# A hybrid decoder layer on one core: the last quarter of attention's loads at unit 28, first cached values behind blocks, a third block result buffer

## The reference, cut to what matters

```
PATTERNS = ((128, 1), (512, 4), (2048, 16))          # window, dilation
s = einsum(q, k) * scale + bias[t5_bucket(rel * dil)]  # masked: 0 <= rel <= span
m = max(s); pr = exp(s - m); den = sum(pr)
o = pr @ v / den;  lse = m + log(den)
out = sum(softmax(stack(lse)) * stack(o))              # over the three patterns
# sample: keys and values = cache (2048 rows) followed by the 8 new rows
```

## Time and profile before

| | us |
|---|---|
| median of three runs (lowest, highest) | 2499.04 (2494.27, 2503.16) |
| span of the profiled execution | 2491.6 |
| PE busy (share of the span) | 2197.5 (88%) |
| DVE, ACT, POOL busy | 851.4, 564.0, 288.6 |
| mean of the 16 DMA engines | 176 GB/s |

### The profile page before, as it was taken

How to read it: one execution, slowest core, us unless ns; L and a number is a source line. 1 busy time by engine, 2 the same in 40 slices (tenths; PEclk the granted TensorE clock), 3 DMA queues, 4 the chain that set the end, 5 groups by cost and what they waited for, 6 DMA issues and landing times. The chain is left out here.

```text
span 2491.6 us, 27646 instructions
## 1 busy us (share of the span) xinstructions
PE 2197.5 (88%) x7615; PEld 1096.3 (44%) x7616; DVE 851.4 (34%) x1969; ACT 564.0 (23%) x1111; POOL 288.6 (12%) x463
## 2 busy tenths in 40 slices
PE   4996999998896577899999749999999999999995
PEld 1343555444453244455544324444444444444442
DVE  4566643036542223454566531111111111111111
ACT  3410101235532122333432201111111111111111
POOL 0001020001001010000021121111111111111111
PEclk8998999999997677899999969999999999999998
DMA  9152141433448543222244344676659788687873
GB/s 378 74 216 49 54 91 40 149 101 98 139 156 213 165 152 155 67 85 83 79 160 178 103 166 155 226 254 193 197 174 344 259 322 320 220 327 274 292 266 69
DMA packets 122756, 438.91 MB, mean 176 GB/s; under 512 B 31955, under 2 KB 70579, under 8 KB 102115
## 3 DMA queue, kind: packets, MB, share of 16 engines
q1 hardware_dynamic: 92520, 309.99, 34.0%
q0 software_dynamic: 26032, 112.64, 16.7%
q10 hardware_dynamic: 4112, 15.14, 1.5%
HBM read 356.39 MB, written 83.10 MB: 176 GB/s over the span
## 5 line engine op out<-in xcount | busy, mean ns | idle before, releaser
L2528 PE MATMUL bank<-arena 128*128 128x512 f32 x1120 | 492.1, 596 | 14.4 <-issue 14.4
L2179 PE MATMUL bank<-arena 128*128 128x512 f32 (+1 forms) x960 | 359.7, 534 | 9.6 <-ACTq L1050 9.6
L2528 PEld LDWEIGHTS bank<-arena 128*128 128x128 f32 x1120 | 212.4, 190 | 290.2 <-issue 290.2
L2556 PE MATMUL bank<-arena 128*128 128x512 f32 x560 | 250.4, 600 | 9.4 <-issue 9.4
L2179 PEld LDWEIGHTS bank<-arena 128*128 128x128 f32 x960 | 168.7, 192 | 194.4 <-issue 193.5
L2433 PE MATMUL bank<-arena 128*128 128x512 f32 x512 | 248.5, 615 | 2.2 <-DMA arena<-mix_d 2.2
L2071 DVE COPY arena<-bank 128x512 f32<-128x512 f32 x50 | 34.6, 693 | 548.7 <-PE bank L2543 548.7
L2556 PEld LDWEIGHTS bank<-arena 128*128 128x128 f32 x560 | 103.6, 190 | 133.3 <-issue 130.3
L2338 PE MATMUL bank<-arena 128*128 128x64 f32 x568 | 95.5, 301 | 41.1 <-DVEq L1810 27.9
L2433 PEld LDWEIGHTS bank<-arena 128*128 128x128 f32 x512 | 90.2, 193 | 76.5 <-issue 74.0
L2081 DVE TENSOR_TENSOR arena<-bank,arena 128x512 f32<-128x512 f32 (+1 forms) x50 | 34.5, 690 | 256.4 <-PE bank L2556 208.6
(11 more groups left out here) (476 smaller groups left out, 2548.7 us busy)
## 6 DMA issues: line engine op xcount, KB each, us to landing
arena<-wg SPq DMA_DIRECT2D x32, 2048.0 KB
arena<-wu SPq DMA_DIRECT2D x32, 2048.0 KB, 15.2
arena<-wd SPq DMA_DIRECT2D x32, 2048.0 KB, 8.6
arena<-mod_w SPq DMA_DIRECT2D x12, 2048.0 KB, 18.3
z_d<-arena ACTq DMA_DIRECT2D x12, 1056.0 KB, 6.5
arena<-z_d POOLq DMA_DIRECT2D x10, 1056.0 KB, 7.6
arena<-kc POOLq DMA_DIRECT2D x8, 1280.0 KB, 8.4
arena<-vc POOLq DMA_DIRECT2D x8, 1280.0 KB, 8.0
```

Of the source, the lines that this page charges most:

```text
L2179: ins = mm(bank[n % 2][:, 0:w], wz[:, i % 3, k, :], hT[:, k, t0:t0 + w], start=(k == 0), stop=(k == KT - 1))
L2528: ins = mm(bank[bk][:, :], xgT[:, s, k, :], m[w][:, k, :], start=(k == 0), stop=(k == KT - 1))
L2556: ins = mm(bank[4 + h][:, :], hhT[:, k, :], wd[w][:, k, 512 * h:512 * h + 512], start=(k == 0), stop=(k == 3))
```

## The change

- `ldq 3`, the last quarter of queries, keys and values, moves from behind the barrier into the slot of unit 28. It waits in addition for `t1_ready`, since part of `v1` first holds a bias table.
- `ost` gets a third tile, in the place of a weight that is no longer needed (`gatew`). `att_max` of block b now waits for the store of block b-3, and there is a third semaphore, `st_att2`; the reader of `att_d` waits for all three.
- POOL's loads stand in another order: keys 2 and 3 come ahead of values 0 and 1, and these two wait until one and two blocks more are done (`att_o` of 2 and 3).

```diff
--- before.py
+++ after.py
@@ -136,6 +136,7 @@
             a, w = VCOLS[name]
             return vec[:, a:a + w] if i is None else vec[:, a + i:a + i + 1]
 
+        gatew_at = top[0]
         gatew = take(4 * P).rearrange("p (n m) -> p n m", n=4)
         lg = take(NT * 36).rearrange("p (i n) -> p i n", i=NT)
         zero = lg.rearrange("p i n -> p (i n)")[:, 0:512]
@@ -191,7 +192,8 @@
         top[0] = h_at
         ssb = take(2048).rearrange("p (n k) -> p n k", n=4)
         pt = take(2048).rearrange("p (n k) -> p n k", n=4)
-        ost = take(2 * 264).rearrange("p (n h c) -> p n h c", n=2, h=4)
+        ost = [take(264), take(264), take(264, gatew_at)]
+        ost = [o.rearrange("p (h c) -> p h c", h=4) for o in ost]
         kc_at = top[0]
         wo = take(8192).rearrange("p (k n) -> p k n", k=KT)
         kc = take(2 * 2560, kc_at).rearrange("p (n h k) -> p n h k", n=2, h=2)
@@ -328,7 +330,7 @@
                     *tile(3), ("tabs", 0), ("Ap", 0), ("As", 0), *tile(4), *tile(5), ("A", 1), ("Aw", 1), *tile(6), ("tabs", 1), ("Ap", 1), ("As", 1), *tile(7),
                     ("sqA",), ("B", 0), *tile(8), ("outA",), ("outAn",), *tile(9), ("tabs", 2), ("B", 1), *tile(10), ("sqB",), *tile(11), ("outB",),
                     ("outBn",), *tile(12), *tile(13), ("ldq", 0), *tile(14), ("ldq", 1), ("t1p",), *tile(15), ("ldq", 2), *tile(16), *tile(17), *tile(18),
-                    ("bar", 1), ("ldq", 4), ("ldq", 3), ("smp",)]
+                    ("bar", 1), ("ldq", 4), ("smp",)]
 
         BLOCKS = []
         for c in range(4):
@@ -346,7 +348,7 @@
         VPART = ((0, 4), (4, 8), (8, 11))
 
         def sample(u):
-            out = [("qb",)] if u == 4 else []
+            out = [("qb",)] if u == 4 else [("ldq", 3)] if u == 28 else []
             if u in (28, 56):
                 out.append(("so", u // 28 - 1))
             hf, n = divmod(u, 28)
@@ -624,6 +626,8 @@
 
             def ldq(step, c):
                 t0, w = CHUNKS[c]
+                if c == 3:
+                    sp.wait_ge(S("t1_ready"), 1)
                 if c == 0:
                     sp.wait_ge(S("st_mixd"), 16 * 6)
                     for h in range(4):
@@ -646,7 +650,7 @@
                 if u % 4 == 3:
                     bk = u // 4
                     sp.wait_ge(S("att_o"), bk + 1)
-                    sp.dma_start(att_rows(bk), ost[:, bk % 2].rearrange("p h c -> p (h c)")).then_inc(S(f"st_att{bk % 2}"), 16)
+                    sp.dma_start(att_rows(bk), ost[bk % 3].rearrange("p h c -> p (h c)")).then_inc(S(f"st_att{bk % 3}"), 16)
 
             def smp_out(step, hf):
                 sp.wait_ge(S("smp_o"), hf + 1)
@@ -657,8 +661,8 @@
                 if i >= 2:
                     sp.wait_ge(S("mrg_o"), i - 1)
                 if i < NT - 1:
-                    for q in range(2):
-                        sp.wait_ge(S(f"st_att{q}"), 64 * (i // 4 + 1))
+                    for q in range(3):
+                        sp.wait_ge(S(f"st_att{q}"), 16 * len(range(q, 8 * (i // 4 + 1), 3)))
                     sp.dma_start(ma[:, i % 2].rearrange("p q h c -> p q (h c)"),
                                  att_d[:, t0:t0 + P].rearrange("q t c -> t q c")).then_inc(S(f"ld_ma{i % 2}"), 16)
                 else:
@@ -871,6 +875,8 @@
                 def values(b):
                     if b >= 2:
                         pool.wait_ge(S("smp_pv"), b - 1)
+                    else:
+                        pool.wait_ge(S("att_o"), 2 + b)
                     pool.dma_start(vc[:, b % 2], A["vc"][b]).then_inc(S(f"ld_vc{b % 2}"), 16)
                     pool.dma_start(vn[0:8, b % 2], O["v"][TP + 8 * b:TP + 8 * b + 8]).then_inc(S(f"ld_vc{b % 2}"), 16)
                 def tables():
@@ -883,7 +889,7 @@
                 keys(0)
                 keys(1)
                 tables()
-                for f, b in ((values, 0), (values, 1), (keys, 2), (keys, 3), (keys, 4), (keys, 5), (values, 2), (values, 3),
+                for f, b in ((keys, 2), (keys, 3), (values, 0), (values, 1), (keys, 4), (keys, 5), (values, 2), (values, 3),
                              (values, 4), (values, 5), (keys, 6), (keys, 7)):
                     f(b)
                 pool.dma_start(rw, A["rw"]).then_inc(S("ld_wo"), 16)
@@ -1214,8 +1220,8 @@
             def att_exp(step, u):
                 w = 128 * len(BLOCKS[u // 4][4])
                 act.wait_ge(S("att_max"), u + 1)
-                link(act.activation(ssb[:, u % 4, 0:w], ssb[:, u % 4, 0:w], ACT.Exp, bias=ost[:, (u // 4) % 2, u % 4, 64:65], scale=-1.0,
-                                    accum_out=ost[:, (u // 4) % 2, u % 4, 65:66]))
+                link(act.activation(ssb[:, u % 4, 0:w], ssb[:, u % 4, 0:w], ACT.Exp, bias=ost[(u // 4) % 3][:, u % 4, 64:65], scale=-1.0,
+                                    accum_out=ost[(u // 4) % 3][:, u % 4, 65:66]))
                 act.sem_inc(S("att_exp"), 1)
 
             def att_turned(step, u):
@@ -1783,12 +1789,12 @@
                 if u == 0:
                     dve.wait_ge(S("ld_t1"), 16 * 8)
                     dve.wait_ge(S("t1_ready"), 1)
-                if u % 4 == 0 and u >= 8:
-                    dve.wait_ge(S(f"st_att{(u // 4) % 2}"), 16 * (u // 8))
+                if u % 4 == 0 and u >= 12:
+                    dve.wait_ge(S(f"st_att{(u // 4) % 3}"), 16 * (u // 12))
                 if u >= 4:
                     dve.wait_ge(S("att_pT"), u - 3)
                 dve.wait_ge(S("att_s"), u + 1)
-                m = ost[:, (u // 4) % 2, u % 4, 64:65]
+                m = ost[(u // 4) % 3][:, u % 4, 64:65]
                 link(dve.tensor_tensor_reduce(out=ssb[:, u % 4, 0:w], in0=bank[u % 2][:, 0:w], in1=tab[:, tab.shape[1] - w:],
                                               scale=-1.0, scalar=3e38, op0=ALU.add, op1=ALU.min, accum_out=m))
                 dve.sem_inc(S("att_max"), 1)
@@ -1806,7 +1812,7 @@
                 if u % 4 == 3:
                     bk = u // 4
                     dve.wait_ge(S("att_pv"), u + 1)
-                    link(dve.tensor_copy(ost[:, bk % 2, :, 0:64], bank[4][:, 0:256].rearrange("p (h c) -> p h c", h=4)))
+                    link(dve.tensor_copy(ost[bk % 3][:, :, 0:64], bank[4][:, 0:256].rearrange("p (h c) -> p h c", h=4)))
                     dve.sem_inc(S("att_o"), 1)
 
             def sample_queries(step):
```

## The result

The changed kernel took 2477.16 us, the median of four runs (2469.26 to 2479.55), beside 2501.1 us of the kernel before on the same chip: ratio 0.9903, 95% interval 0.9884 to 0.9922, some 24 us less. A second set of runs on another occasion gave 2469.09 beside 2499.8 us, 0.9871 (0.985 to 0.9892). The profiled span went from 2491.6 to 2473.0 us, and in the second pair of profiles from 2487.7 to 2470.5 us: 18.6 and 17.2 us, less than the medians say. The kernel before was profiled at the quick end of its runs both times: its second profiled run took 2489.42 us, while none of the seven runs beside it was under 2495.54.

What follows compares the result with a forecast made beforehand. It took PE's 21.89 us stand before unit 8, for block 0's store behind the seven loads, as the one large gap. 20.9 + 2.0 + 3.1 = 26.0 us off 2499.0 gave 2473 us, range 2462 to 2488.

Steps and rivals of the forecast that it cites:

- The gap before unit 8: Before unit 8's transposes, PE idle 21.89 us for block 0's late store; moved loads and third tile save 20.9 us.
- the twin: Units 36 to 41, same work as units 8 to 13: 19.00 us against 39.90, so the store cost 20.9 us.
- Keys 0 and 1: PE's 2.04 us wait for cached keys at 808.30 us goes once the seven loads are away: 2.0 us saved.
- Keys 2 and 3 ahead of the values: Next in line at unit 11; landing as keys 6 and 7 do, 8.9 us, already in the 19.00 us: nothing added.
- The waits of values 0 and 1: Value 1, issued after block 2, lands by 871.5 us, wanted at 873.56: costs nothing, 2 us or more to spare.
- The seven loads at unit 28: Done near 913 us, block 6's store near 915, wanted at unit 36 by 921.2: 6 us slack, no cost.
- rival A: Stall moves to unit 36, block 6's store behind the seven loads: up to 18 us, likely 2482 us; chance 0.10.
- Later blocks: Third tile removes the 1.55 and 1.57 us waits before the transposes of units 32 and 56: 3.1 us saved.
- Rival C: With fewer idle stretches, two of four windows reach full clock: 8.6 us more saved, 2464 us; chance 0.07.
- B: Gap shrinks but keys 2 and 3 or value 1 land late: 5 to 10 us come back, 2481; chance 0.08.
- D: Slower than before: loads at unit 28 starve stores, units 36 and 40 both wait, up to 2509 us; chance 0.03.
- The signs: Right if no att_d wait over 2 us before unit 56, store 0 landing under 8 us, units 8 to 13 18–21 us.

Runs made afterwards that it cites:

- e1: Kernel before with only the seven loads moved to unit 28, two tiles, POOL's old order: units 0 to 56 177.9 us, ratio 0.9952.
- e3: Kernel before with only POOL's new order and its waits, loads at the barrier, two tiles: units 0 to 56 184.9 us, ratio 0.9976.
- e7: Changed kernel with the seven loads at unit 6, right behind the store of block 0: units 0 to 56 173.1 us, ratio 0.9924.
- e5: Changed kernel without the third tile: units 0 to 56 170.4 us, ratio to the kernel before 0.9949.
- e6: Changed kernel with POOL's old order, without the waits on blocks: units 0 to 56 169.8 us, ratio to the kernel before 0.9927.
- e8: Changed kernel with quarter 2 also moved, to unit 28, and the last quarter to unit 60: units 0 to 56 167.4 us, ratio 0.9898.
- e9: Changed kernel with the seven loads at unit 60 in place of 28: units 0 to 56 166.4 us, ratio to the kernel before 0.9915.
- e2: Kernel before with only the third result tile, loads at the barrier, POOL's old order: units 0 to 56 181.1 us, ratio 0.9944.
- e4: Changed kernel with the seven loads left behind the barrier: units 0 to 56 174.2 us, ratio to the kernel before 0.994.
- e10: Changed kernel with POOL's new order but without the waits of values 0 and 1: units 0 to 56 166.3 us, ratio 0.9909.

## Why the prediction was right

It said 2473 us from 2499, 26 us off. By the first set of runs it is 24 us, by the second 31, by units 0 to 56 it is 26.4 and 22.3 us in the two pairs of profiles. The mechanism of its main term, 20.9 of the 26 us, held; the terms around it were off in both directions.

The span it forecast, 2465.6 us, was missed by 7.4 and 4.9 us. The time came out closer because the 7.4 us that it added from span to median weren't a fixed distance: in every listed run that was profiled, time and span differ by 1.7 to 1.8 us, and the rest was, as far as the record tells, the quick run that was profiled before. Two errors partly cancel here, which is luck.

- *The gap before unit 8.* Predicted 20.9 us by the twin, measured 22.0 and 19.9 in units 8 to 14. The cause is shown by e1, e3 and e7: the store stood behind the seven loads in SP's queue. POOL's queue set how long that took: the two queues moved the same number of packets in 820 to 826 us (268 and 270), but 2.02 against 0.20 MB. That 22.0 is above 20.9 goes with the clock of that profile. The prediction gave the move and the tile together as the cure; e5 shows that, with POOL's new order, the move does it alone, and that the tile's work lies at unit 32. With POOL's old order the tile still brings 3.0 us in units 8 to 14 (e1 to e6).
- *Keys 0 and 1.* Predicted 2.0 us. The wait is gone in the first profile only. In it the cached scores begin 1.9 us earlier, counted from unit 0, and 0.4 us go again in longer busy times. In the second PE still stood 1.08 us for the keys, where the kernel before stood 1.62 us, and e8 and e9 show 1.17 and 0.82 us: keys 0 and 1 can be late without the seven loads too. Units 0 to 8 are 1.5 and 0.4 us shorter. This term was sized too high. The second pair, before, then changed:

```profile
808.81 3.63 PE L2358 MATMUL bank<-arena 128*32 128x512 f32 x8 [1.62 <-DMA arena<-kc]
...
809.32 3.63 PE L2364 MATMUL bank<-arena 128*32 128x512 f32 x8 [1.08 <-DMA arena<-kc]
```


- *Keys 2 and 3 ahead of the values.* Right, and undersized in its weight: called "the cover this edit keeps" and priced at nothing in the sum, it is worth 2.4 to 4.6 us beside the other two parts (e6), and in e2, e4 and e7 these keys are the longest wait left, 14.3, 8.8 and 7.5 us. PE's idle there, 1.68 and 1.23 us, is near the twin's 0.82.
- *The waits of values 0 and 1.* Priced at nothing, and nothing in either direction (e10).
- *The seven loads at unit 28.* The store of block 6 was put at 915 us on the old time axis, some 890.5 us on the new; it landed at 890.8. SP took 3.8 us for the issues, not the 15.8 us that rival A feared, and unit 36 comes at 897.8 us. The slack of 6 us was real (7.0 us measured), and without the third tile PE stands 4.54 us there and units 28 to 36 take 3.7 us more (e5). That the landing fits to 0.3 us is luck in part. The working let 1.0 MB of the loads go before POOL's values; in the trace q1 had moved 2.2 MB by 883 us, all or nearly all of them, since q0 moved its first bytes only after 880 us. It was the store itself that then crept beside q0: q1 moved 0.15 MB in 883 to 889 us, at the 0.03 MB per us of the working.
- *Later blocks.* Predicted 3.1 us; units 28 to 36 and 36 to 56 give 1.9 and 2.0 us. Both waits for stores are gone, but not all of their idle time: before unit 32's transposes PE still waits 0.67 us for ACT, in place of 1.55. Before unit 56's it waits 0.64, in place of 1.57, but that place lies behind unit 56's scores, outside the 1.9 and 2.0 us. So the stores account for 0.6 and 0.4 us of these, in units 28 to 36. The rest is PE's busy time, 35.10 us before and 33.59 after in units 42 to 56, at a clock of 0.78 and 0.81, and no part of the working.
- *Rival C*, the clock, came true in one of its four windows, units 8 to 14, with 0.91 and 0.81 in the two profiles in place of the twin's 0.73. Against the twin of the same trace that is some 1 us, not 8.6. The other windows kept 0.60 to 0.73. A, B and D did not occur.
- *The signs.* No wait for `att_d`, and units 8 to 14 as said. The store of block 0 landed after 8.3 and 8.7 us, not under 8; units 0 to 8 took 19.3 and 20.8 us, not 18.8. From unit 56 to the end the changed kernel took 7.7 and 4.1 us longer, of which the experts' part 3.1 and 2.9 us, which the prediction had called a sign of being wrong. Over fourteen profiles that part lies between 1016.3 and 1022.4 us; why is open.

## What to carry to other kernels

A small store that others wait for should not stand behind large loads in its engine's DMA queue, above all while another queue is full (26.1 and 27.3 us to land here, in place of 8.3 and 8.7). Ask for every bulk load when it is first read, and put it behind the stores that are due before that. Where several parts each shorten the same wait, their single gains (here 13.7, 10.5 and 6.7 us) don't add up to the joint one (26.4, or 24.2 by the second profile): the next late transfer sets what each is worth.

## What the runs showed that was not expected

- A store of 132 KB behind no load of its own queue still took 8.3 us with the bias tables in flight, and 11.9 us with two loads of 1280 KB on POOL's queue, against 1.7 us in the calmest rows.
- SP's issue of the seven loads took 15.8 us at the barrier, where the DMA engines were busy all the time, 8.3 us at unit 6 (e7), and 3.8 us at unit 28, where they were 78% busy.
- The length of 484 us of identical instructions varies by 7.5 us from profile to profile, mostly in PE's busy time, which is a third of what the change brought. A difference of spans between two single profiles is no measure of a change of this size.
